# Strassen's form for the down projection in the last MLP group of both layers, with the seams between layers turned round

## What is computed

```python
for i in range(DEPTH):                      # DEPTH = 2
    hn = rms_norm(h, norm_mix_g[i])
    h = h + (fox_mixer(...) if i % 2 == 0 else gla_mixer(...))
    h = h + sqrelu_mlp(rms_norm(h, norm_mlp_g[i]), mlp_w_up[i], mlp_w_down[i])
return rms_norm(h, norm_final_g)

def sqrelu_mlp(h, w_up, w_down):            # [512,1024] x [1024,4096], then x [4096,1024]
    return jnp.square(jax.nn.relu(h @ w_up)) @ w_down
```

## Time and profile before

| | us |
|---|---|
| median of 3 runs | 1194.52 (1193.46 to 1194.93) |
| the profiled execution's own time | 1195.42 |
| its span on the core | 1193.3 |
| TensorE busy (matmuls) | 1166.9, 98% |
| VectorE busy | 747.0, 63% |
| ScalarE busy | 534.0, 45% |
| GpSimd busy | 42.1, 4% |
| DMA | 119.04 MB, mean 100 GB/s |

### The profile page before, as it was taken

The page is one execution under the profiler, slowest core; times in us unless marked ns, Lnnn a source line. Parts: engine busy times, 40 slices in busy tenths (PEclk is TensorE's granted clock), DMA queues, the critical chain, the costliest instruction groups (busy, mean ns, idle before and its releaser), DMA issues.

```text
span 1193.3 us, 14650 instructions
## 1 busy us (share of the span) xinstructions
PE 1166.9 (98%) x5677; PEld 974.0 (82%) x5677; DVE 747.0 (63%) x950; ACT 534.0 (45%) x764; POOL 42.1 (4%) x90
## 2 busy tenths in 40 slices
PE   6999999999999999999999999999999999999997
PEld 5788888888788788888878988987887888878886
DVE  5547878636866957864357675493468478487532
ACT  6346667436535535443345333243454354454332
POOL 2000000000000000000020101100000000000001
PEclk9999999999999999999999999999999999999999
DMA  9257655433071251353220330214022514215301
GB/s 285 49 96 159 136 130 151 134 104 106 5 237 41 71 176 35 121 196 106 71 73 14 94 107 1 72 38 134 19 93 76 172 36 160 87 35 177 105 18 71
DMA packets 116138, 119.04 MB, mean 100 GB/s; under 512 B 38929, under 2 KB 84017, under 8 KB 116082
## 3 DMA queue, kind: packets, MB, share of 16 engines
q1 hardware_dynamic: 112992, 116.21, 32.9%
q10 hardware_dynamic: 3090, 2.05, 0.6%
HBM read 103.50 MB, written 2.10 MB: 88 GB/s over the span
## 4 chain that ended last, share of the span: by engine, by line
PE 84%; DVE 7%; issue 4%; ACT 3%; DMA 1%; SPq 0%; POOL 0%; DVEq 0%; POOLq 0%; ACTq 0%
PE bank L1041 8%; PE bank L1045 8%; PE bank L1044 8%; PE bank L1170 7%; PE bank L1175 6%; PE bank L1174 6%; PE bank L1028 6%; PE bank L1032 6%; PE bank L1031 6%; PE bank L1254 2%; PE bank L1258 2%; PE bank L1257 2%; DVE w_stage L1640 2%; PE bank L1424 2%; ACT w_hi L642 2%
## 5 line engine op out<-in xcount | busy, mean ns | idle before, releaser
L1028 PE MATMUL bank<-hT_lo,w_hi 128*128 128x512 f32 x512 | 199.8, 390 | 0.0
L1032 PE MATMUL bank<-hT_hi,w_lo 128*128 128x512 f32 x512 | 199.3, 389 | 0.0
L1031 PE MATMUL bank<-hT_hi,w_hi 128*128 128x512 f32 x512 | 199.2, 389 | 0.0
L1626 DVE TENSOR_TENSOR w_lo<-w_stage,w_hi 128x2048 fp32r<-128x2048 f32 x68 | 155.0, 2287 | 48.0 <-ACT w_hi L642 27.3
L642 ACT ACTIVATE w_hi<-w_stage 128x2048 fp32r<-128x2048 f32 x60 | 113.9, 1912 | 112.3 <-PE bank L1170 71.5
L1041 PE MATMUL bank<-w_lo,hT_hi 128*128 128x512 f32 (+1 forms) x320 | 115.0, 359 | 4.4 <-DVE hT_lo L2003 1.9
L1028 PEld LDWEIGHTS bank<-hT_lo,w_hi 128*128 128x128 f32 x512 | 96.1, 188 | 20.6 <-DVE hT_lo L1683 0.5
L1032 PEld LDWEIGHTS bank<-hT_hi,w_lo 128*128 128x128 f32 x512 | 96.1, 188 | 20.0
L1031 PEld LDWEIGHTS bank<-hT_hi,w_hi 128*128 128x128 f32 x512 | 96.1, 188 | 19.6
L1045 PE MATMUL bank<-w_hi,hT_lo 128*128 128x512 f32 (+1 forms) x320 | 111.7, 349 | 0.0
L1044 PE MATMUL bank<-w_hi,hT_hi 128*128 128x512 f32 (+1 forms) x320 | 111.7, 349 | 0.0
(11 more groups left out here) (237 smaller groups left out, 2119.8 us busy)
## 6 DMA issues: line engine op xcount, KB each, us to landing
w_stage<-in_mlp_w_up_dram SPq DMA_DIRECT2D x32, 1024.0 KB, 5.6
w_stage<-in_mlp_w_down_dram SPq DMA_DIRECT2D x32, 1024.0 KB, 5.7
w_stage<-in_fox_w_in_dram SPq DMA_DIRECT2D x32, 256.0 KB, 4.8
w_stage<-in_gla_w_in_dram SPq DMA_DIRECT2D x8, 1024.0 KB, 5.3
w_stage<-in_fox_w_in_dram SPq DMA_DIRECT2D x4, 1024.0 KB, 8.6
qa<-qk_hi SPq DMA_DIRECT2D x32, 128.0 KB
w_stage<-in_fox_w_out_dram SPq DMA_DIRECT2D x4, 1024.0 KB, 5.3
w_stage<-in_gla_w_in_dram SPq DMA_DIRECT2D x8, 512.0 KB, 4.6
```

The costliest lines, as they stand in the source:

```text
L1028: a = pe.matmul(out, w[0][:, k, :], x[1][:, k, :], start=(k == 0), stop=False)
L1031: pe.matmul(out, w[0][:, k, :], x[0][:, k, :], start=False, stop=False)
L1032: a = pe.matmul(out, w[1][:, k, :], x[0][:, k, :], start=False, stop=(k == KT - 1))
L1626: dve.tensor_tensor(w_lo[:, to, :], w_stage[:, at, :], fp(w_hi[:, to, :]), ALU.subtract).then_inc(w_lo_made, 1)
```

## The change

- `WINO = GROUPS - 1` goes; all four groups of both layers are in Strassen's form, and the units, sums and counters are renumbered. In layer 0, TensorE, ACT and DVE run the last group as straight code (`last=True`); in layer 1 TensorE keeps it in its loop.
- A product with n >= 2 goes block by block: all k for t = 0, then all for t = 1, and each block waits for its own `added`.
- Product 0 no longer waits for part 3 of u ahead of its first matmul, but for part k + 1 ahead of each k >= 1.
- On DVE the sum T3 is made ahead of T1's split.
- The order of the last group makes the right half of `h` ready first, so the seam is turned round: the right half is transposed between products 5 and 6 of the last group (`turn_middle_right`), the left after product 6, into banks of their own (`MIDDLE_BANK`); `project_gqk` takes k in the order 4 to 7, 0 to 3 (`ORDER`). The GLA units GLA_U + 1 and + 2, split in the plain group's queue before, are split behind the seam.
- `make_masks` on DVE moves from ahead of group 3 into it, after u's first part. At the end of layer 1 the right half is scaled first and the left last.

```diff
-    for k in range(KT // 2):
-        if n == 0 and k == 0:
-            pe.wait_ge(u_lo_made, g * U_PARTS + (parts + 3))
-        if n < 2 and k == 3:
-            pe.wait_ge(u_lo_made, g * U_PARTS + (parts + 4 + n))
-        for t in range(2):
...
+    places = [(k, t) for k in range(KT // 2) for t in range(2)]
+    if n >= 2:
+        places.sort(key=lambda place: place[1])
+    for i, (k, t) in enumerate(places):
+        if n == 0 and t == 0 and k:
+            pe.wait_ge(u_lo_made, g * U_PARTS + (parts + k + 1))
+        if n == 1 and t == 0 and k == 3:
+            pe.wait_ge(u_lo_made, g * U_PARTS + (parts + 5))
+        if n in (2, 3, 4, 6) and k == 0:
+            pe.wait_ge(added, g * WINO_ADDS + (adds + {2: 1, 3: 3, 4: 5, 6: 9}[n] + t))
...
                     for n in range(len(PRODUCTS)):
                         product(g, n)
+                        if last and n == 5:
+                            turn_middle_right()
+
+                wino(0, ready_late(2 * layer + 1, adds))
+                with pe.Fori(1, GROUPS if layer else GROUPS - 1) as g:
                     wino(g)
-                for j in range(4):
-                    split_of(0, 0, c + j)
...
-                add_rows(0, 0, c + 4, (u_hi, u_lo), lambda kg: pe.wait_ge(u_lo_made, parts + 4 * kg + 4), False,
-                         None if layer else lambda: turn_left(GLA_ADDS, False))
+                if layer == 0:
+                    wino(GROUPS - 1, None, True)
...
+            def turn_middle_right():
+                pe.wait_ge(added, GLA_ADDS - TB)
+                for t in range(TB):
+                    turn_h(2, t, range(KT // 2, KT))
+
+            def turn_middle_left():
+                pe.wait_ge(hT_lo_made, 2 * KT + KT // 2)
+                for t in range(TB - 1):
+                    pe.wait_ge(added, GLA_ADDS - TB + t + 1)
+                    turn_h(2, t, range(KT // 2))
...
# DVE, in a group
                     wino_lo(layer, g, W11)
                     wino_sum(layer, g, T1)
+                    wino_sum(layer, g, T3)
                     wino_lo(layer, g, T1)
                     sums(g, 2)
-                    wino_sum(layer, g, T3)
                     lo(g, 2, A_R1, A_11 + 1, 3)
...
# DVE, end of the last group
+                    if not last:
+                        wino_lo(layer, g, WINO_UNITS + U0)
+                    elif layer == 0:
+                        split_lo(0, 0, GLA_U)
+                    else:
+                        for t in range(TB):
+                            scale_right(t)
                     collect(g, 5)
+                    if last and layer == 0:
+                        late_lo(2, range(KT // 2))
+                    elif last:
+                        left(0)
+                        left(1)
                     collect(g, 6)
+                    if last and layer == 0:
+                        late_lo(2, range(KT // 2, KT))
+                    elif last:
+                        left(2)
+                        left(3)
...
# ACT, after the last group
+                if layer == 0:
+                    late_squares(2, GLA_ADDS, 1)
+                    split_hi(0, 0, GLA_U)
+                    late_hi(2)
+                    late_squares(2, GLA_ADDS, 0)
...
-            split_hi(0, 0, GR_U[0])
+            for unit in range(GLA_U + 1, GR_U[0] + 1):
+                split_hi(0, 0, unit)
```

More of the change, by code:

```diff
@@ L127, in plain @@
 def plain(c):
-    return c < MLP0_U or CLASSIC0_U <= c < MLP1_U or c >= CLASSIC1_U
+    return c < MLP0_U or GLA_U <= c < MLP1_U
 def loaded(c, slot):
-    wino = (c >= CLASSIC0_U) + (c >= CLASSIC1_U)
-    return sum(loads_of(u) for u in range(c + 1) if plain(u) and slot_of(u) == slot) + wino * WINO * LOADS_PER_SLOT[slot]
+    earlier = sum(loads_of(u) for u in range(c + 1) if plain(u) and slot_of(u) == slot)
+    return earlier + (c >= GLA_U) * GROUPS * LOADS_PER_SLOT[slot]
 def wino_loaded(layer, unit):
@@ L687, in last_norm, with late_hi @@
[L687 to L698, removed]
-                                       accum_out=ss[:, half, t:t + 1]).then_inc(squared, 1)
-                squares(0)
-                for k in range(KT):
-                    act.wait_ge(h_turned, (n - 1) * KT + k + 1)
-                    act.activation(hT_hi[:, k, :], bank[turn_bank(k, early)][:], ACT.Copy,
+            def late_hi(n):
+                for i, k in enumerate(ORDER[n]):
+                    act.wait_ge(h_turned, (n - 1) * KT + i + 1)
+                    act.activation(hT_hi[:, k, :], bank[turn_bank(n, k)][:], ACT.Copy,
@@ L751, in mlp @@
                     hi(g, 3, A_R1, A_S4 + 1, True)
-                    for unit in (T2, W22, T3, W21, T4):
+                    for unit in (T2, W22, T3):
                         wino_hi(layer, g, unit)
-                    c_next = c + WINO_UNITS
+                    if last and layer:
+                        act.wait_ge(w_lo_made, g * WINO_UNITS + (c + W22 + 1))
+                        act.dma_start(fgain, norm_final_g.partition_broadcast(P)).then_inc(fgain_loaded, 16)
+                    wino_hi(layer, g, W21)
@@ L1181, in wino @@
+                def wino(g, first=None, last=False):
                     for unit in range(4):
@@ L1697, in add_slots @@
-            def add_slots(i, per, c, adds, ends=False, splits=4, early=False, late=None, scaled=False,
-                          out_of=None):
-                for j in range(4):
-                    if out_of is not None and j == 1:
-                        wino_lo(out_of, 0, U0)
-                    elif j < (splits if out_of is None else 1):
-                        split_lo(i, per, c + j + 3)
-                    if late is not None and j == 3:
-                        late_lo(late, range(KT // 2), early)
+                dve.tensor_tensor(to, bank[sum_bank(half, t, early)][:], to, ALU.add).then_inc(added, 1)
@@ L1710, in add_slots @@
-                            if ends and j == 3 and t:
-                                right(t - 1)
-                        if ends:
-                            if j == 1:
-                                for t in range(TB):
-                                    scale_left(t)
-                            else:
-                                right(TB - 1)
+                            add(j // 2, t, adds + 4 * (j // 2) + t + 1, layer == 0)
             def mlp(layer, c, adds):
@@ L1894, in _ @@
                     keep_qk(head + 3)
[L1895 to L1896 removed]
+            add_slots(FOX_OUT_U, FOX_ADDS, 1, 0)
+            late_lo(1, range(KT // 2, KT))
             mlp(0, MLP0_U, MLP0_ADDS)
[L1900 removed]
+            for unit in range(GLA_U + 1, GR_U[0] + 1):
+                split_lo(0, 0, unit)
             dve.wait_ge(z_done, 1)
```

296 lines of the change are left out of this document (130 added, 166 removed).

## The result

The changed kernel took 1180.76 us (median of 4 executions, 1178.45 to 1183.01) against 1194.72 of the kernel before on the same chip: ratio 0.9872, 95% interval 0.9851 to 0.9894. The four are 1178.45, 1178.74, 1182.78 and 1183.01, so the median lies between two pairs, where no execution is. The profiled execution is the longest of the four, 1183.01 us with a span of 1181.2.

What follows compares the result with a forecast made beforehand. TensorE was taken to bound the MLPs. Terms -10.9 - 3.5 - 1.4 + 0.5 = -15.3 from the profiled 1195.42 gave 1180.1, and 0.9 less for the median 1179.2 us; range 1176.8 to 1182.2.

Steps and rivals of the forecast that it cites:

- Matmuls: Last MLP group of each layer: Strassen form takes 24 matmuls fewer per group, 48 x 0.227 = -10.9 us.
- The formula: Matmul price N / 2.4 + 2.5 ns, 0.216 us for 512 columns; by it the matmul term would be 10.4.
- Product 0's wait: Start of product 0 in six Strassen groups: the 0.59 us stall for u_lo goes, -3.5 us, margin 2.3.
- Product 2's wait: Start of product 2: only the first add is awaited; 6 x 0.30 - 8 x 0.05 = -1.4 us.
- New work and masks: New Strassen groups' sums and collects, and layer 0's masks in a 5.41 us VectorE gap: nothing new waits, 0.
- The seam: Passage from layer 0's MLP to GLA: two more unit splits on VectorE delay zT and the gate matmuls, +0.5 us.
- The end: After the last product: same add, square, rsqrt, scaling and store; 0, between -0.3 and +0.3 us.
- The stalls stay: Rival: an earlier TensorE waits elsewhere on VectorE's packed queue, so only the matmuls count; 1184.1 us, chance 0.10.
- The seam did not queue up: Rival at the seam: three slow VectorE splits make gate matmuls wait, +2.4 instead of +0.5; 1181.1 us, chance 0.13.
- W22's load was never late: Rival: early sum T3 blocks VectorE's queue waiting for W22's load; 1206.4 us with the load at 12 us, chance 0.02.
- The clock rival: Rival: the clock's dip behind GLA goes, -1.6 us more; 1177.6 us, chance 0.13.
- the clock falls at a new place: Sign that the forecast is wrong: TensorE's clock falls where it had not before; no size or chance given.

Runs made afterwards that it cites:

- e1: The changed kernel with all three wait edits undone, leaving the 48 fewer matmuls and turned seams; 1186.46 us, ratio 0.993 to the kernel before.
- e5: The changed kernel with T3's sum back behind T1's split on VectorE; 1180.36 us, one execution.
- e3: The changed kernel with products n >= 2 run k by k, waiting for both adds of the collect; 1187.81 us, one execution.
- a0: The changed kernel run again without edits, to see how its executions spread; its own time is not given.
- a1: The changed kernel run again without edits on another chip; its own time is not given.
- c1: The changed kernel plus four unused matmuls ahead of the last gate tile, gates' wait left open; 1180.59 us profiled, three others 1178.05 to 1178.68.
- e4: The changed kernel with product 0 again asking for u's third part ahead of its first matmul; 1180.43 us, one execution.
- f1: The changed kernel plus four unused matmuls in TensorE's wait ahead of the gate matmuls; none of 4 executions long, median not given.

## Why the prediction was right

**The sum.** 1179.2 was forecast, 1180.76 measured, within the range of 1176.8 to 1182.2; the twelve executions of the changed kernel have a median of 1179.4. Without the clock's part the table gives 15.37 us against the 15.3 of the sum. For the time itself there was luck: two of the four executions are long, and at 1182.78 and 1183.01 they lie above the range; with three of them so would the median.

- *Matmuls, -10.9:* 48 fewer, steps still 0.227 apart. e1's MLPs show it within 0.2 us once their added stalls are allowed for. Right. The formula that the prediction sets beside the row is, in the Trainium skill (TensorE: Matmul & The Clock Gate, "Back-to-back issue gap"), called the gap of a single isolated matmul. The term was taken from the row and doesn't hang on it.
- *Product 0's wait, -3.5:* gone, with the margin as worked out (2.4 for 2.3). Right; and e5 shows that it doesn't hang on the earlier T3, of which the prediction said no more than that it does no harm.
- *Product 2's wait, -1.4:* 0.11 us left in a middle group where 0.05 was put, and up to 0.23 in a layer's last group. The waits together gave 2.1 in each MLP where the prediction had 2.45. Slightly too high. The mechanism, two sides that meet, was right, and e3 shows how near it was: asking for both adds loses 0.75 to 0.90 there.
- *New work and masks, 0:* the masks run from 528.28 to 533.04 and VectorE idles 0.80 before the block sums. Right.
- *The seam, +0.5:* it cost 0.0. The term that was too high is the price of the two added splits, put between 2.29 and 3.09 each from the earlier trace rows. 7.49 us for three is one slow split of 3.1 and two whose starts are 2.2 apart: the first, beside GpSimd's reading operation of 604.79, is slow; the second, beside its memsets from 606.97 on, is not. The trace agrees with the Trainium skill (SBUF — State Buffer, "Who interferes with whom"), by which an instruction that only writes does not contend.
- *The end, 0:* -0.26, inside the 0.3 that was allowed. The prediction doesn't say that block order is what keeps it there: k outermost costs 1.6.

VectorE's timeline of the masks, last one and what follows, on which the fourth point rests:

```profile
528.28 0.28 DVE L1796 TENSOR_TENSOR gate_w<-gate_w 128x128 int32<-128x128 int32 x1
...
532.75 0.29 DVE L1801 SCALAR_TENSOR_TENSOR masks<-gate_w,ge 128x128 uint8<-128x128 int32 x1
533.84 0.43 DVE L1713 TENSOR_TENSOR u_raw<-u_raw 128x256 f32<-128x256 f32 x1 [0.80 <-ACT u_raw L717]
```

**The rivals.** "The stalls stay" is refuted for the kernel, and true for e3's version of it. The seam did not queue up, and W22's load was never late (T1's and T3's sums run back to back in all eight groups, at most 0.1 us apart). The clock rival had the right subject and missed half of it: the dip behind GLA does come and go between executions (worth 1.6 us, as worked out), but the dearer case was a dip at a second place, 3.3 us in a third of the executions. The prediction named "the clock falls at a new place" only among what would make it wrong and gave it no chance; the range held the median by being 3 us wide upward, but not the long executions. A wait of TensorE that ends in slow steps in one trace should have made every such wait a candidate, the 0.87 us of the earlier trace rows first.

## What to carry to other kernels

When waits follow one another on the engine that bounds the kernel, mending the first hands its time to the next: cost them as a chain, each with its own margin, and judge an edit by what all of them leave. An order in which outputs finish one after the other, block by block, helps twice, since the next consumer can start on the first block, and only one block's tail stands behind the last matmul. Compare kernels stage by stage from fixed events and not by totals: two of these totals were off by a clock dip of 1.6 us in a place that the edit had not touched.

## What the runs showed of the hardware

- The same wait of 0.87 us ahead of the gates was followed by the full clock in some executions and by half of it in others. Its length does not decide, nor does its moment in the span: gate matmuls that started at 612.75 (a0) dipped and those at 612.77 (e5) did not. Counted from the clock's first rise these two lie 1.1 us apart (598.40 and 599.53), and by that count the three at 598.4 have the dip and the four with an open wait at 599.1 to 599.9 have none. That count is what 14 profiles show, not an experiment.
- The 1.88 us behind GLA likewise: dips in the profiles of before, changed, a0, a1, c1 and e5, none in e1 to e4 and f1. A difference in GLA between two single profiles says nothing about an edit.
- Halving the clock costs the gates more than their own time: 0.84 us in the eight matmuls, and the rest of the 3.3 in the eleven steps behind them, up to 621.94. The first of these, beside the end of the gates, takes 1.21 us and the next nine 0.43 each.
